# The output projection cut in two by its input, and other places for ScalarE's and GpSimd's work, in a two-layer trunk of hybrid mixers

## The reference

```python
h = x
for layer in range(2):
    hn = rmsnorm(h, mix_norm[layer])
    # layer 0: sliding-window attention and mLSTM; layer 1: SSD and RWKV-7
    h = h + mixer(hn @ w_in) @ w_out           # w_in 1024 x 2312 or 1024 x 3336, w_out 1024 x 1024
    h = h + square(relu(rmsnorm(h, mlp_norm[layer]) @ w_up)) @ w_down     # width 4096
return rmsnorm(h, final_norm)
```

## Time and profile before

| | us |
|---|---|
| median of 3 runs | 1441.8 (1441.53 to 1442.5) |
| the profiled execution | 1446.55 |
| its span | 1444.7 |
| TensorE busy | 1355.6 (94%) |
| GpSimd busy | 653.6 (45%) |
| VectorE busy | 587.0 (41%) |
| ScalarE busy | 541.5 (37%) |

### The profile page before, as it was taken

One profiled execution on the slowest core, in us unless ns is written; L12 is line 12 of the kernel. 1 busy time (PEld: TensorE's weight loads), 2 busy tenths in 40 slices (PEclk: granted clock), 3 DMA queues, 4 the chain that ended last, 5 costly groups with the idle time before them and its releaser, 6 DMA issues.

```text
span 1444.7 us, 17744 instructions
## 1 busy us (share of the span) xinstructions
PE 1355.6 (94%) x6427; PEld 1089.8 (75%) x6427; DVE 587.0 (41%) x966; ACT 541.5 (37%) x883; POOL 653.6 (45%) x801
## 2 busy tenths in 40 slices
PE   5999967999999999999899997998799999999998
PEld 4777646788888888886578776888678888888886
DVE  4537575421211212345599376355442122121233
ACT  4346643441322323337444425332334132241332
POOL 5653213564555645553345321211265555455562
PEclk9999978999999999999799988999999999999999
DMA  8322101323323333232122210000033233332321
GB/s 268 88 76 65 50 1 29 103 88 93 98 88 100 89 97 92 87 102 59 44 73 73 59 59 15 1 2 1 29 92 98 88 96 94 89 100 87 102 88 59
DMA packets 202131, 109.13 MB, mean 76 GB/s; under 512 B 4570, under 2 KB 199376, under 8 KB 201936
## 3 DMA queue, kind: packets, MB, share of 16 engines
q1 hardware_dynamic: 201648, 108.16, 25.8%
q0 software_dynamic: 416, 0.07, 0.0%
HBM read 106.11 MB, written 2.10 MB: 75 GB/s over the span
## 4 chain that ended last, share of the span: by engine, by line
PE 75%; DVE 6%; ACT 3%; issue 2%; POOL 0%; DVEq 0%; ACTq 0%; POOLq 0%
PE ps L825 21%; PE ps L826 21%; PE ps L827 21%; PE ps L812 2%; PE ps L1192 1%; DVE late L2397 1%; PE ps L1206 1%; PE ps L1119 1%; PE ps L1245 1%; PE ps L1217 1%; PE ps L1080 0%; PE ps L1260 0%; PE ps L1258 0%; PE ps L1235 0%; ACT arena L1582 0%
## 5 line engine op out<-in xcount | busy, mean ns | idle before, releaser
L747 POOL TENSOR_TENSOR w_lo<-raw_w,w_hi 128x256 fp32r<-128x256 f32 x760 | 618.2, 845 | 639.3 <-ACT w_hi L1311 639.3
L1311 ACT ACTIVATE w_hi<-raw_w 128x1024 fp32r<-128x1024 f32 x190 | 201.2, 1059 | 594.5 <-PE ps L827 447.7
L825 PE MATMUL ps<-hn_hi,w_hi 128*128 128x512 f32 x880 | 360.8, 410 | 3.4 <-POOL w_lo L747 2.5
L826 PE MATMUL ps<-hn_lo,w_hi 128*128 128x512 f32 x880 | 352.8, 401 | 0.0
L827 PE MATMUL ps<-hn_hi,w_lo 128*128 128x512 f32 x880 | 352.4, 400 | 0.0
L825 PE MATMUL ps<-hid_hi,w_hi 128*128 128x512 f32 x640 | 254.2, 397 | 1.1 <-DVE hid_lo L1795 1.1
L826 PE MATMUL ps<-hid_lo,w_hi 128*128 128x512 f32 x640 | 253.8, 397 | 0.0
L827 PE MATMUL ps<-hid_hi,w_lo 128*128 128x512 f32 x640 | 253.7, 396 | 0.0
L825 PEld LDWEIGHTS ps<-hn_hi,w_hi 128*128 128x128 f32 x880 | 168.4, 191 | 53.4 <-issue 11.3
L826 PEld LDWEIGHTS ps<-hn_lo,w_hi 128*128 128x128 f32 x880 | 168.4, 191 | 42.4 <-issue 3.1
L827 PEld LDWEIGHTS ps<-hn_hi,w_lo 128*128 128x128 f32 x880 | 168.2, 191 | 41.2
(11 more groups left out here) (363 smaller groups left out, 1339.4 us busy)
## 6 DMA issues: line engine op xcount, KB each, us to landing
raw_w<-in_w_up SPq DMA_DIRECT2D x64, 512.0 KB, 4.0
raw_w<-in_w_down SPq DMA_DIRECT2D x64, 512.0 KB, 3.6
raw_w<-in_o_w_in SPq DMA_DIRECT2D x27, 512.0 KB, 3.8
raw_w<-in_e_w_in SPq DMA_DIRECT2D x19, 512.0 KB, 3.7
raw_w<-in_e_w_out SPq DMA_DIRECT2D x8, 512.0 KB, 4.0
raw_w<-in_o_w_out SPq DMA_DIRECT2D x8, 512.0 KB, 3.5
rwkv_raw<-in_x SPq DMA_DIRECT2D x4, 512.0 KB, 8.3
out<-arena SPq DMA_DIRECT2D x8, 256.0 KB, 2.9
```

Of the source, the lines that this page charges most:

```text
L747: nc.gpsimd.tensor_tensor(w_lo[:, n % CUT, ks], raw_w[:, n % RING, ks], w_hi[:, n % CUT, ks].bitcast(F32), ALU.subtract).then_inc(w_cut, 1)
L825: mm(o, a_hi, b_hi, start=(k == 0), stop=False)
L826: mm(o, a_hi, b_lo, start=False, stop=False)
L1311: A(w_hi[:, n % CUT], raw_w[:, n % RING], ACT.Copy).then_inc(w_high, 1)
```

## The change

1. *The output projection in halves.* Its first four slots are no longer four tiles of 1024 x 128 but four of 512 x 256: two for the first 512 inputs (tiles 0 and 1, tiles 2 and 3), two for the last 512. `half_tile` makes 12 products; the lower halves of tiles 0 to 2 stand ahead of the transposes of y_ml or y_rw, that of tile 3 behind them, then come the four upper halves and the four tiles that are left whole. Tiles 0 to 3 hold PSUM banks 0 to 3 meanwhile, and the turned blocks banks 4 to 7. A half slot's successor waits for the new semaphore half_done.
2. *High and low parts.* The first four blocks are split early: in layer 0 in chunk 2 of the mLSTM loop, on ScalarE and on VectorE (`low_first`), in layer 1 in chunk 3, straight from the PSUM banks of y_ssm. The last four are split from PSUM as well, without the copy to `y_mix`.
3. *The front of layer 1.* lora 1 to 3, kk_sum, kk_inv, sub, bonus and a_turn stand a slot later on TensorE, and gates, decays, root and block copies on ScalarE with them; VectorE's order follows.
4. *Between the front and the chunks.* VectorE's two transposes of the inverse (L2391, L2392) move ahead of `take_staged(21)`, and a new semaphore inv_ready tells ScalarE of them. z_tok's transposes stand behind rv_tok. ScalarE fills the inverses first, then copies v_tok, then does z_tok's Silu and the sigmoid.
5. *y_ssm.* Its squares, root and eight products move from chunk 0 to chunk 1, its transposes to the head of chunk 3.
6. *Zeroing.* GpSimd does all memsets of inv_t, inv_d and inv_p. k_tok, g_tok and others get other places in memory.

The core of the diff:

```diff
-    behind = {0: [("norm", 2), ("norm_tok",)], 1: [("turn", ("dt",))], 3: [("lora", 0), ("lora", 1)],
-              4: [("lora", 2), ("lora", 3), ("a_cum",)], 6: [("kk_sum",)], 7: [("kk_inv", f) for f in range(4)],
-              8: [("sub", 0)], 9: [("sub", 1), ("sub", 2)], 10: [("sub", 3)], 12: [("bonus",)], 13: [("a_turn",)],
+    behind = {0: [("norm", 2), ("norm_tok",)], 1: [("turn", ("dt",))], 3: [("lora", 0)],
+              4: [("lora", 1), ("lora", 2), ("a_cum",)], 5: [("lora", 3)], 7: [("kk_sum",)],
+              8: [("kk_inv", f) for f in range(4)], 9: [("sub", 0)], 10: [("sub", 1), ("sub", 2)], 11: [("sub", 3)],
+              13: [("bonus",)], 14: [("a_turn",)],
...
+    def put_mixed(layer, turned):
+        for j in range(4):
+            put("out", layer, j, bank=j)
+        for f in range(4):
+            put(turned, f, bank=4 + f)
...
+            def half_tile(layer, j, upper_half):
+                n = base["out", layer] + 2 * upper_half + j // 2
+                o = bank(("out", layer, j)) if upper_half else free(pe, "out", layer, j)
+                c = slice(j % 2 * SW, (j % 2 + 1) * SW)
+                for q in range(4):
+                    k = 4 * upper_half + q
+                    pe.wait_ge(w_cut, PARTS * n + q + 1)
+                    if j == 0:
+                        operand_ready(3 * layer + 1)(k)
+                    a_hi, a_lo = hi_half[:, n % CUT, q, c], lo_half[:, n % CUT, q, c]
+                    mm(o, a_hi, hid_hi[:, k, :], start=(k == 0), stop=False, skip_group_check=True)
+                    mm(o, a_hi, hid_lo[:, k, :], start=False, stop=False, skip_group_check=True)
+                    ins = mm(o, a_lo, hid_hi[:, k, :], start=False, stop=(k == KT - 1), skip_group_check=True)
+                if upper_half:
+                    close(ins, "out", layer, j)
+                elif j % 2:
+                    ins.then_inc(S["half_done"], 1)
...
+                for j in range(3):
+                    half_tile(0, j, 0)
                 pe.wait_ge(S["y_ml_gated"], NT - 1)
                 pe.wait_ge(S["y_ml_ready"], 1)
                 for f in range(4):
                     turn(("y_ml", f), [o_gate[:, n, f * P:(f + 1) * P] for n in range(NT)])
+                half_tile(0, 3, 0)
...
+            def cut_turned(turned):
+                cut_next()
+                if turned == "y_rw":
+                    full(act, turned, 3)
                 for f in range(4):
...
+                    o = full(act, turned, f)
+                    A(hid_hi[:, 4 + f, :], o, ACT.Copy).then_inc(high, 1)
+                cut_next()
...
+                if n == 2:
+                    for k in range(4):
+                        low_first(0, k, y_mix[:, k, :])
                 ml_combine(n)
```

More of the change, by code:

```diff
@@ L231, in rwkv_chunks @@
     for n in range(NT):
+        yield "z_tok", n
+    for n in range(NT):
+        if n == NT - 1:
+            for f in range(4):
+                yield "y_ssm", f
         for half in range(2):
@@ L242, in rwkv_chunks @@
         if n == 0:
-            for f in range(4):
-                yield "y_ssm", f
             yield "rk_tok", 0
@@ L326, in make_plan @@
                         put("inter", n, par)
-            for f in range(4):
-                put("y_ml", f)
+            put_mixed(0, "y_ml")
         else:
@@ L358, in make_plan @@
                 put(*item)
-            for f in range(4):
-                put("y_rw", f)
-        for j in range(KT):
+            put_mixed(1, "y_rw")
+        for j in range(4, KT):
             put("out", layer, j, bank=j)
@@ L1748, in _ @@
             ln_root(NT - 1)
-            for f in range(4):
-                drained(act, "y_ssm", f)
-            cut_mixed("y_rw")
+            cut_turned("y_rw")
             project_out(1)
@@ L1806, in project_out @@
             def project_out(layer):
-                low_mixed(layer)
+                low_turned(layer, "y_ml" if layer == 0 else "y_rw")
                 for k in range(KT):
```

217 lines of the change are left out of this document (121 added, 96 removed).

## The result

Eight timed runs of the changed kernel have their median at 1432.59 us (1428.64 to 1436.41), eight of the kernel before, beside them, at 1442.45 (1441.51 to 1448.77): a ratio of 0.9916, 95% interval 0.9898 to 0.9933. By the ratio the kernel is 0.84% faster, some 12 us; the two medians lie 9.9 us apart. Either is less than half of the 26.4 that were forecast, and 1432.6 lies outside the range of 1406 to 1426.

What follows compares the result with a forecast made beforehand. TensorE, busy 94% of the span, bounds the kernel, so only its waits and low-clock stretches can shrink. 5.9 - 0.5 + 10.4 + 1.0 + 9.6 = 26.4 us, against the median 1441.8 makes 1415.4 us; range 1406 to 1426.

Steps and rivals of the forecast that it cites:

- Layer 0's end: Half tiles fill TensorE's 11.2 us wait ahead of y_ml's transposes: gain 5.9 us, bounds 4 and 8.
- So y_ml is ready at 226.3 + 2.5 = 228.8: Layer 0's end: VectorE's four low parts (2.49 us) now stand in the chain that ends with y_ml.
- Rival 2: Chunk 1: GpSimd's affine steps and memsets slow VectorE's ssm_norm products, 4 to 5 us lost, memsets another 3: 1423; 16%.
- The second front: Layer 1's front: kk_sum's wait goes, waits come ahead of kk_inv and slot 17: loss 0.5 us, gain 8 to loss 4.
- Chunk 0: First chunk behind the second front: earlier masks and pt, y_ssm's transposes gone: gain 10.4 us, bounds 6 and 11.5.
- Chunks 1 to 3: Later chunks: moved memsets and ssm_norm cost nothing, y_ssm's transposes fill chunk 3's wait: gain 1 us, loss 1 to gain 2.
- Layer 1's end: Three half tiles fill the 6.5 us wait ahead of y_rw's transposes: gain 9.6 us, bounds 7.5 and 10.
- The last y product ends at 1015.0 at PEclk 1.00: Layer 1's end: starting point at full clock, from which the half tiles take 8.4 us and end at 1023.4.
- the clock may stay up: Chunk 3, at pt: y_ssm's transposes fill TensorE's 2.6 us wait; part of the 1 us gain.
- (1): Second front: the 5.1 and 2.5 us waits vanish with nothing replacing them, 8 us more gain, 1407; 14%.
- (3): Layer 0: a PSUM bank or half slice comes late, half tiles run behind y_ml, 6 us back, 1421; 5%.
- (4): Second front: ScalarE's joint chain exceeds 5.6 us on slots 6 to 19; at 2.5 us per slot, 1450; 4%.

Runs made afterwards that it cites:

- the second pair: The changed kernel and the kernel before, both unchanged, run once more for second profiles: 1431.49 us (ratio 0.9913) and 1445.01 us (1.0003).
- the fourth half tile: Changed kernel with old front, cut held back, one half tile in last chunk, and layer 0's fourth half tile ahead of y_ml's transposes: 1414.15 us, ratio 0.9793.

## Why the prediction was wrong

The direction was right, and where the work moved it did what was said of it; of the 26.4 us less than half arrived. Three terms of the sum came out worse than forecast, each by a mechanism that it left out. By its steps:

**Layer 0's end** (5.9 forecast, 3.9 measured, 4.7 in the second pair). The half tiles ran as forecast, the clock too. The step that failed is "So y_ml is ready at 226.3 + 2.5 = 228.8". It counted the four low parts and left out that the cut of the next half slice moves into this stretch as well: its four subtractions on GpSimd overlap the last gating steps and add 1.3 + 0.4 us to them, as holding the cut back showed. The low parts themselves took 2.98 us instead of 2.49. The trace of before had a row to price it by: its last four gating steps take 2.14 us beside GpSimd's product, the four ahead of them 1.11 without.

```profile
222.21 1.11 DVE L2055 TENSOR_SCALAR late<-late,small 128x128 f32<-128x128 f32 x4
...
223.45 2.14 DVE L2055 TENSOR_SCALAR late<-late,small 128x128 f32<-128x128 f32 x4
```

Rival 2 had this mechanism at another place, chunk 1. There it came too, with 3.8 us added, and cost TensorE nothing.

**The second front** (-0.5 forecast, -1.8 measured, -1.5 in the second pair). Its picture came true almost row by row: the wait of 6.3 us ahead of kk_inv (at 702.2), none ahead of kk_sum, and the late slice 17 behind the bonus copy, the table load and the Silu. Not foreseen was the wait of 2.2 us for slot 8's slice (at 690.0). Mis-sized was "TensorE gets slice 17 some 2.5 us late": it was 4.0, and the slot itself then took 7.2 us, partly at the lower level, instead of 5.7. What was missing was the bound: VectorE, busy for 30.5 of the 32 us from 765 on in the kernel before. With that row read, a lead of TensorE ahead of it could have been seen to be worth little, and idle time that the new order gives VectorE is hard to win back (in the changed kernel it is busy for 26.3 us of the same window: it waits there for ScalarE). Set against the changed kernel with the old front, the new order costs 5 to 7 us. The comparison with the kernel before hides most of it, since the old order took 3 us more there; part of that is clock level (its last slots ran at the lower level in the first profile, two slots at 802 us in the second), the rest is open. How much VectorE's bound holds alone was not tested.

**Chunk 0** (10.4 forecast, 10.5 measured). The step that held best, by its rows: d stands where it was forecast, 18.4 us behind ssd_back(3). That the number fits to 0.1 is partly luck, for the second pair of profiles gives 8.1 (the transposes of y_ssm, which leave this place, cost the kernel before 3.43 us in the one and 1.97 in the other). Zeroing on GpSimd carries 2.9 us of the step. Even the next bound was the one named: d waits 3.2 us for what VectorE takes from pt behind the products with z_tok. A memset on GpSimd took 0.95 us, below the 1.2 taken, and did not slow VectorE: in after a product of two SBUF inputs takes 0.68 us beside it, where in the kernel with the zeroing on VectorE it takes 1.21 beside GpSimd's subtractions.

```profile
871.59 0.68 DVE L2406 TENSOR_TENSOR arena<-arena,rows 128x512 f32<-128x512 f32 x1
...
871.06 0.95 POOL L798 MEMSET late<- 128x1024 f32 x1
```

```profile
872.91 1.21 DVE L2393 TENSOR_TENSOR arena<-arena,rows 128x512 f32<-128x512 f32 x1
```

The rule weighed in the prediction is that of the Trainium skill (SBUF — State Buffer, "Who interferes with whom"): a GpSimd instruction that only writes SBUF does not contend with a VectorE instruction of two SBUF inputs. These rows agree, and so do the 0.48 us of ssm_norm's products beside the memsets of chunk 1.

**Chunks 1 to 3** (1.0 forecast, 0.9 measured, 0.7 in the second pair). Right in sum. "The memsets that leave VectorE stood in its idle time: nothing" held only of the old order: with ssm_norm in chunk 1 they would cost 2.1 us there.

**Layer 1's end** (9.6 forecast, 3.7 measured) is the largest miss. The step was "The last y product ends at 1015.0 at PEclk 1.00", from which all was counted with the y products at full clock. In chunk 3 the waits ahead of pt and d no longer lowered the clock; it fell later, at 996, behind waits of 0.7, 1.8, 0.3 and 0.9 us, so that the y products took 8.6 us instead of 4.7 and the first nine steps of the halves 0.43 us each: 3.9 and 1.9 us lost, together 5.8 of the 5.9 that are missing. Filling one or two of the waits kept the clock up (four kernels of four). The forecast had written down that "the clock may stay up" at pt, and not asked what that changes behind it. The value of the halves themselves, 6.7 us by the profile and 7 by the ratios, is also below the 9.6. The lower level there belongs to the change and is no accident of one execution: both profiles of after have it, and neither profile of before.

**The clock between executions.** The sum was taken from one profiled execution to a median. Executions of the changed kernel lie up to 8 us apart, with a mean granted clock of 0.970 in the fastest and 0.961 to 0.963 in the slowest. The gain is 17.2 us in one pair of profiles, 15.9 in the second pair of spans, and 12 by the ratio of all runs. That the difference is the clock is likely and not shown, as no execution of after near 1436 us has a trace. One place where such time goes is seen: the front of layer 1 in its new order takes 229.2 us in its fastest profile and 232.5 in its slowest, with nearly the same waits (ahead of kk_inv 6.3 us in six of the seven, 4.8 in one). The likeliest value had no room for it, and the range took in too little.

**The rivals.** The front did not gain (1): the wait for kk_sum went, but the late slice stayed (2.6 us) and longer waits came. GpSimd's interference (2) was there, 3.8 us where 8.3 were feared, and stayed within the room. The half tiles started at once (3), 215.44 against the end of the last inter product at 215.5. Nor was the kernel slower (4).

## What to carry to other kernels

When work is moved to fill a wait, follow what its operands and its slot free up: here it was the next weight slice, whose cutting on GpSimd came to lie beside the very chain that TensorE was waiting for. Before TensorE is given a lead in a stretch, look in the windows whether another engine is dense there; if so, the lead is worth little, and idle time given to that engine is hard to win back. Count a saving at the clock of the stretch in which it will run, and treat short waits that are filled as worth more than their length: the fourth half tile gave 2.3 us, more than the 0.5 to 1.4 expected, since the transposes behind the shortened wait then ran at the full clock (1.94 us instead of 3.26). And a term read from one pair of profiles holds no better than the clock level that each of them had there: chunk 0's gain is 10.5 us in one pair and 8.1 in the other.

## What was not expected of the hardware

TensorE's granted clock can fall in work that follows only short waits: in the changed kernel it fell from 1.00 to 0.50 at about 996 us, with TensorE busy for 10.8 of the 12 us before and its longest wait there 0.9 us, and it did so at the same place in both profiles. Products of 64 to 128 columns fill that stretch; with a half tile of twelve 512-column products between pt and d it stayed at 1.00.

VectorE's TENSOR_SCALAR, with a single tensor input of 128 columns, is held up by GpSimd as its products of two inputs are. Four of them take 1.11 us with GpSimd idle (225.33), 2.13 to 2.14 beside one GpSimd product of 1.26 us (the kernel that holds the cut back, and the kernel before), and 3.41 beside that product and the subtractions behind it, while GpSimd's instructions keep their 1.26 and 2.77 us. The Trainium skill (SBUF — State Buffer, "Who interferes with whom") has tensor_scalar among the operations that can take the shared pair of ports, with the loser blocked for the whole of the other's instruction; the added 1.0 us beside a product of 1.26 fits that.
